# Sample tokens' expert rows added at slabs 226 to 268 of each layer in place of 226 to 284

## The chip, the cores and the metric

The kernel runs on one core of a Trainium2 chip. The metric is the device time of one execution in microseconds (us); the figure given is the median of 3 runs. The core's engines have names of their own in the profile: PE does matmuls (PEld loads their weights), DVE, ACT and POOL work on tiles, and SP issues DMAs. Each runs its own list of instructions in order and waits on semaphores for the others. 16 DMA engines move data between HBM and the on-chip memory for all queues together.

## The reference

Two layers of a hybrid decoder run over 256 prompt tokens and 32 sample tokens (8 sequences of 4), with 1024 channels, in float32. Each layer is a token mixer (a recurrent block in layer 0, a convolution block in layer 1) and then a PEER channel mixer, which picks 128 of 16,384 experts for every token (8 heads by 16) and adds up their rows of a table V, weighted:

```python
def expert_block(args):
    xblk, iblk, gblk = args
    u = jnp.take(u_tab, iblk, axis=0)
    act = jax.nn.gelu(jnp.einsum('ted,td->te', u, xblk).astype(jnp.float32))
    w = (gblk * act).astype(xblk.dtype)
    v = jnp.take(v_tab, iblk, axis=0)
    return jnp.einsum('te,ted->td', w, v)
```

## The kernel before

**The stream.** All weights and both expert tables flow through the core once, as 592 slabs of 128x1024 float32 (0.52 MB), 296 per layer: 16 for the mixer's input, 8 for its output, 16 for the PEER queries, 128 of U, 128 of V. `layer_slabs` (L60) sets their order: slabs 40 to 135 are U, then come 32 of V and 32 of U, and from slab 200 to 295 only V. The V slabs are read in visits, mostly of two slabs for two rows of experts; the visits of the last two of three blocks of experts begin at slabs 200 and 264 (`BLOCK_START[1]`, `BLOCK_START[2]`). For the prompt tokens every expert is computed densely and weighted by a gate that is zero where it was not picked.

**One slab.** SP issues its DMA into one of 3 buffers of `land` (L446), once the slab three before has been split. ACT makes the upper part `w_hi` (`split`, L583), DVE the rest `w_lo` (`split_lo`, L1470; POOL at L533 for a few early slabs), both in rings of 4. PE multiplies w_hi and w_lo with the weights `g_hi` and `g_lo`: 12 matmuls of 128x512 per V slab (`v_slab`, L909 to L911). ACT rounds g_hi for a visit (L783), DVE makes g_lo (L1745). The loops of ACT and DVE run over the slabs r of a layer. At r they split slab r + 3, and they make g_hi and g_lo of a visit at the r just before its first slab: w_lo is made three slabs ahead of PE, g_lo one.

**The gates.** DVE makes one-hot tiles for a few tokens at a time (`onehots`, L1592 and L1597), PE expands them into gates (`expand`, L956), DVE multiplies these into `hidden` (`apply`, L1609). `gate_schedule` (L115) spreads 64 such chunks a layer; those of the last block fall on slabs 200 to 242.

**The sample tokens.** Their picks don't go through the dense gates. Each layer has 32 adds (`SMP`): in add k, each of 128 partitions takes one picked row of V, 1024 wide, times its weight, and adds it to `smp_acc` (`add_sample`, L1659; the first is L1668, the others L1671). The rows come by `fetch_samples` (L505) on POOL: two indirect DMAs a row, one per half (L524), into 7 buffers in `hidden`. Rows 0 to 6 wait until a visit has freed their buffer (DVE's g_lo of that visit), each later row k waits for add k - 7. On POOL layer 0's `wide_weights` (L495) stand behind the last fetch. The adds are placed by the list `ADD_AT` (L150); in DVE's loop over r they come last:

```python
for r in range(first, SLABS):
    while applied < GATES and ONEHOTS_AT[applied] + 2 <= r: ...   # apply
    if r + 1 in VISITS: ...                                       # g_lo of the next visit
    split_lo(base + r + LEAD)
    while made < GATES and ONEHOTS_AT[made] <= r: ...             # onehots
    while fetched < SMP and ADD_AT[fetched] <= r:
        add_sample(L, fetched)
        fetched += 1
```

At slab 285 (`SMP_SUM`) PE sums `smp_acc` over partitions, at slab 287 (`SMP_OUT`) DVE adds the sum to x. Neither place depends on ADD_AT.

**Beside it.** At slab 264 of layer 0 ACT issues two DMAs for layer 1, the keys and the convolution states, 2 MB together (L806, L807). In layer 1 there are none.

Of the kernel before, what the change touches and what calls it, by code (L numbers as in the profile page):

```python
# [83 lines left out]
SLABS = len(LAYER)  # L84
# [10 lines left out]
def block_of(r):  # L95
    return next(b for b, (lo, hi) in enumerate(BLOCKS) if lo <= LAYER[r][2] < hi)


BLOCK_START = [min(r for r in V_AT if block_of(r) == b) for b in range(len(BLOCKS))]
# [46 lines left out]
STORE_LAG = 7  # L146
SMP_LANDS = 7
ACC_SLOT, LAND_SLOT, YT_SLOT = 32, 36, 72
ADD0, ADD1 = BLOCK_START[1] + 26, SLABS - 12
ADD_AT = [ADD0 + k * (ADD1 - ADD0) // (SMP - 1) for k in range(SMP)]  # L150
SMP_SUM, SMP_OUT = SLABS - 11, SLABS - 9
TURN_LATE = SLABS - TWICE
# [1734 lines left out]
```

How the kernel before makes its waits and increments, by code:

```python
        @block.sync  # L439
        def _(sp):
            for n in range(TOTAL):
                if n >= LANDS:
                    ready, count = lo_ready(n - LANDS)
                    sp.wait_ge(ready, count)
                place = n // SLABS * SLABS + LAYER[n % SLABS][1]
                sp.dma_start(land[:, n % LANDS, :], stream[place]).then_inc(landed[n % LANDS], 16)
                if n == 0:
                    for k in range(4):
                        two = slice(2 * k, 2 * k + 2)
                        sp.dma_start(x[:, two, :], x0[:, two, :]).then_inc(x_in[k], 16)
                        if k == 0:
                            sp.dma_start(cols[:, :], cols_d).then_inc(loaded, 16)
                for c in range(CH):
                    if n == SLABS + IN0 + 2 * c + 8:
                        sp.wait_ge(packed, c + 1)
                        sp.dma_start(cfs_d[:, c], packs[c]).then_inc(stored, 16)
                L, r = divmod(n - STORE_LAG, SLABS)
                if r in U_INDEX and U_INDEX[r] % GROUP == GROUP - 1:
                    e = U_INDEX[r] - GROUP + 1
                    for k in range(2):
                        sp.wait_ge(evacuated[k], L * USES + USE_U + U_INDEX[r] // 2 + 1)
                    at = e % STAGE
                    sp.dma_start(act_d[L][:, e:e + GROUP, :], smp_stage[:, at:at + GROUP, :]
                                 ).then_inc(smp_stored[at // GROUP], 16)
# [144 lines left out]
                def used(r):  # L609
                    act.wait_ge(slab_used, base + r + 1)
```

## Time and profile before

| what | value |
|---|---|
| median of 3 runs | 2098.67 us (2096.07 to 2100.24) |
| the profiled execution's own time | 2098.75 us |
| its span, first to last instruction | 2096.9 us |
| granted TensorE clock, mean | 0.995 |
| PE busy | 2055.7 us (98% of the span) |
| DVE busy | 1635.7 us (78%) |
| ACT busy | 960.7 us (46%) |
| POOL busy | 339.8 us (16%) |
| DMA traffic | 358.34 MB, mean 171 GB/s |

The median is the number to predict; the profile is one execution of the same program. Times in a trace row are us from the span's start, and a name such as L1671 is a line of the kernel. `w_lo<-land,w_hi` reads: written from land and w_hi. Buffers that lie in `hidden` (row buffers, smp_acc) have that name. A row's bracket gives the idle time just before it and what ended that. Layer 0's slab 226 is met by DVE at about 820 us, layer 1's at about 1882 us.

### The profile page before, as it was taken

Reading aid. Unit: us, or ns where it says so; the run is one execution under the profiler, and the core shown is the slowest. Engines: PE = TensorE matmul, PEld = TensorE weight load, DVE = VectorE, ACT = ScalarE, POOL = GpSimd, SP = SyncE. Lnnn points to the kernel's source line nnn. Section 1 sums busy time; section 2 is a strip of 40 time slices with the busy share of each in tenths; the row PEclk is TensorE's granted clock in tenths of the full one; section 3 lists DMA queues with packets and bytes.
Section 4 is the critical chain, followed back from the end, with each engine's and each line's share of the span. In section 5 each row is a group of like instructions: output and inputs, shape, how many; then the busy total and the mean of one; then the engine's idle time right before and its main releaser. Section 6 shows DMA issues by size and latency. Waiting matters only on the chain.

```text
span 2096.9 us, 40394 instructions
## 1 busy us (share of the span) xinstructions
PE 2055.7 (98%) x16458; PEld 1889.3 (90%) x16458; DVE 1635.7 (78%) x3068; ACT 960.7 (46%) x1642; POOL 339.8 (16%) x245
## 2 busy tenths in 40 slices
PE   8999999999999999999999999999999999999998
PEld 7899999999889988887897999999998899888886
DVE  7887995555887688978799779965557777789776
ACT  5654553344433343445655545533334433444443
POOL 0014000000000064642110050000000000456420
PEclk9999999999999999999999999999999999999999
DMA  5354554444554457897322435544445544567873
GB/s 180 111 156 130 178 158 157 154 154 157 171 171 147 145 163 233 293 316 230 125 90 65 145 123 163 170 156 154 148 157 172 171 147 147 163 228 259 301 245 103
DMA packets 112935, 358.34 MB, mean 171 GB/s; under 512 B 17264, under 2 KB 27760, under 8 KB 112496
## 3 DMA queue, kind: packets, MB, share of 16 engines
q1 hardware_dynamic: 99888, 319.99, 47.2%
q0 software_dynamic: 12288, 33.60, 4.9%
q8 instruction: 131, 2.15, 0.4%
q10 hardware_dynamic: 576, 2.18, 0.3%
q14 instruction: 52, 0.43, 0.1%
HBM read 349.09 MB, written 6.63 MB: 170 GB/s over the span
## 4 chain that ended last, share of the span: by engine, by line
PE 84%; DVE 12%; ACT 2%; issue 2%; DMA 1%; SPq 0%; DVEq 0%; ACTq 0%
PE ps L878 15%; PE ps L879 14%; PE ps L880 14%; PE ps L909 11%; PE ps L910 10%; PE ps L911 10%; PE ps L956 6%; DVE w_lo L1470 2%; DVE work L1356 2%; DMA land<-stream_dram 1%; ACT w_hi L583 1%; PE ps L1037 1%; DVE hidden L1356 1%; DVE work L1364 0%; DVE hidden L1376 0%
## 5 line engine op out<-in xcount | busy, mean ns | idle before, releaser
L1470 DVE TENSOR_TENSOR w_lo<-land,w_hi 128x1024 fp32r<-128x1024 f32 x562 | 684.8, 1219 | 275.3 <-ACT w_hi L583 274.7
L583 ACT CAST w_hi<-land 128x1024 fp32r<-128x1024 f32 x592 | 621.2, 1049 | 441.1 <-PE ps L911 351.0
L878 PE MATMUL ps<-act_hi,w_hi 128*128 128x288 f32 x2688 | 809.2, 301 | 12.8 <-DVE act_lo L1196 5.9
L879 PE MATMUL ps<-act_hi,w_lo 128*128 128x288 f32 x2688 | 794.9, 296 | 0.0
L880 PE MATMUL ps<-act_lo,w_hi 128*128 128x288 f32 x2688 | 791.9, 295 | 0.0
L878 PEld LDWEIGHTS ps<-act_hi,w_hi 128*128 128x128 f32 x2688 | 505.4, 188 | 18.4 <-issue 10.9
L880 PEld LDWEIGHTS ps<-act_lo,w_hi 128*128 128x128 f32 x2688 | 507.7, 189 | 0.0
L879 PEld LDWEIGHTS ps<-act_hi,w_lo 128*128 128x128 f32 x2688 | 506.7, 188 | 1.0
L909 PE MATMUL ps<-w_hi,g_hi 128*128 128x512 f32 x1024 | 404.9, 395 | 3.6 <-DVE g_lo L1745 3.6
L910 PE MATMUL ps<-w_lo,g_hi 128*128 128x512 f32 x1024 | 399.1, 390 | 0.0
L911 PE MATMUL ps<-w_hi,g_lo 128*128 128x512 f32 x1024 | 398.8, 389 | 0.0
L827 ACT ACTIVATE hidden<-ps 128x256 f32<-128x256 f32 x256 | 98.3, 384 | 497.9 <-PE ps L880 497.6
L512 POOL DMA_INDIRECT smp_act<-act_d,smp_idx x64 | 77.8, 1215 | 1108.3 <-DMA act_d<-smp_stage 1089.4
L909 PEld LDWEIGHTS ps<-w_hi,g_hi 128*128 128x128 f32 x1024 | 192.2, 188 | 44.3 <-DVE w_lo L1470 3.4
L911 PEld LDWEIGHTS ps<-w_hi,g_lo 128*128 128x128 f32 x1024 | 192.2, 188 | 40.6
L910 PEld LDWEIGHTS ps<-w_lo,g_hi 128*128 128x128 f32 x1024 | 192.4, 188 | 37.8
L524 POOL DMA_INDIRECT hidden<-stream_dram,smp_idx x128 | 170.9, 1335 | 162.1 <-DVE hidden L1671 91.1
L1592 DVE TENSOR_TENSOR work<-work 128x512 bf16<-128x512 bf16 (+2 forms) x256 | 164.5, 684 | 0.0
L1609 DVE TENSOR_TENSOR hidden<-ps,hidden 128x512 f32<-128x512 f32 x128 | 88.2, 689 | 95.4 <-PE ps L956 94.4
L956 PEld LDWEIGHTS ps<-work 128*128 128x128 bf16 x4608 | 131.2, 97 | 23.0 <-issue 14.1
L956 PE MATMUL ps<-work 128*128 128x32 bf16 (+1 forms) x4608 | 145.1, 182 | 2.3 <-DVE work L1597 2.3
L1597 DVE TENSOR_TENSOR work<-work 128x512 bf16<-128x512 bf16 x384 | 139.2, 416 | 0.0
(214 smaller groups left out, 1353.8 us busy)
## 6 DMA issues: line engine op xcount, KB each, us to landing
land<-stream_dram SPq DMA_DIRECT2D x592, 512.0 KB
act_d<-smp_stage SPq DMA_DIRECT2D x64, 64.0 KB, 3.3
hidden<-stream_dram,smp_idx POOLq DMA_INDIRECT x128, 5.5
x<-x_dram SPq DMA_DIRECT2D x4, 288.0 KB, 6.8
y_t_dram<-hidden SPq DMA_DIRECT2D x8, 144.0 KB, 1.9
work<-keys_dram SPq DMA_DIRECT2D x1, 1024.0 KB, 7.5
smp_act<-act_d,smp_idx POOLq DMA_INDIRECT x64
work<-keys_dram ACTq DMA_DIRECT2D x1, 1024.0 KB, 9.0
```

The costliest lines, as they stand in the source:

```text
L524: nc.gpsimd.indirect_dma_start(out=smp_land[buf][:, half * 512:half * 512 + 512], out_offset=None, in_=rows, in_offset=bass.IndirectOffset ...
L583: nc.scalar.copy(w_hi[:, m, :], land[:, n % LANDS, :]).then_inc(w_hi_ready, 1)
L878: nc.tensor.matmul(out, w_hi[:, slot, wsl], hi, start=start, stop=False)
L879: nc.tensor.matmul(out, w_lo[:, slot, wsl], hi, start=False, stop=False)
L880: return nc.tensor.matmul(out, w_hi[:, slot, wsl], lo, start=False, stop=stop)
L909: nc.tensor.matmul(out, g_hi[:, ring + ii, tok], w_hi[:, m, row], start=first and ii == 0, stop=False)
L910: nc.tensor.matmul(out, g_hi[:, ring + ii, tok], w_lo[:, m, row], start=False, stop=False)
L911: return nc.tensor.matmul(out, g_lo[:, ring + ii, tok], w_hi[:, m, row], start=False, stop=last and ii == 1)
L956: mm = nc.tensor.matmul(ps[:, GBANK + g % 2, t * n:(t + 1) * n], of_token(j, t), of_token(terms[k], t), start=(k == 0), stop=(k == TERMS - 1))
L1470: V.tensor_tensor(w_lo[:, k, :], land[:, n % LANDS, :], w_hi[:, k, :].bitcast(F32), ALU.subtract).then_inc(lo_by_dve, 1)
L1592: did(V.tensor_tensor(out, keys_of.unsqueeze(1).to_broadcast(shape), per_token(picks_b[:, kind, tok], shape), ALU.is_equal))
L1597: ins = V.tensor_tensor(terms[k], mask, per_token(gate_terms[:, k, tok], shape), ALU.mult)
```

## The change

The end of the range over which the adds are spread moves from 284 to 268; its beginning stays at 226, the number of adds at 32. So ADD_AT was 226, 227, 229, 231, 233, 235, 237, 239, 240, 242, 244, 246, ..., 284 and becomes 226, 227, 228, 230, 231, 232, 234, 235, 236, 238, 239, 240, 242, 243, 244, 246, ..., 268. The fetches from row 7 on hang on the adds and move with them.

```diff
@@ -146,7 +146,7 @@
 STORE_LAG = 7
 SMP_LANDS = 7
 ACC_SLOT, LAND_SLOT, YT_SLOT = 32, 36, 72
-ADD0, ADD1 = BLOCK_START[1] + 26, SLABS - 12
+ADD0, ADD1 = BLOCK_START[1] + 26, SLABS - 28
 ADD_AT = [ADD0 + k * (ADD1 - ADD0) // (SMP - 1) for k in range(SMP)]
 SMP_SUM, SMP_OUT = SLABS - 11, SLABS - 9
 TURN_LATE = SLABS - TWICE
```

## Rows read from the trace of the kernel before

**Rows 1.** The page: PE's busy time, DMA queue q0, the chain that ended last.

```profile
PE 2055.7 (98%) x16458; PEld 1889.3 (90%) x16458; DVE 1635.7 (78%) x3068; ACT 960.7 (46%) x1642; POOL 339.8 (16%) x245
...
q0 software_dynamic: 12288, 33.60, 4.9%
...
PE 84%; DVE 12%; ACT 2%; issue 2%; DMA 1%; SPq 0%; DVEq 0%; ACTq 0%
```

**Rows 2.** Windows, PE alone: stretch, us, busy (matmuls), clock, DMA share, GB/s.

```profile
819.50:882.00 62.50, 62.24 (x566) 1.00 0.74 259
...
932.00:950.00 18.00, 15.43 (x67) 1.00 0.88 330
...
1881.00:1944.00 63.00, 62.73 (x572) 1.00 0.75 258
...
1994.00:2012.00 18.00, 18.00 (x81) 1.00 0.87 282
```

**Rows 3.** Windows, busy PE, PEld, DVE, ACT, POOL; clock, DMA share, GB/s last.

```profile
905.00:932.00 27.00, 27.00 (x121) 22.36 (x120) 22.49 (x22) 13.12 (x15) 12.35 (x11) 1.00 0.90 297
...
1967.00:1994.00 27.00, 27.00 (x121) 22.37 (x120) 21.68 (x21) 13.13 (x15) 12.88 (x11) 1.00 0.89 312
```

**Rows 4.** The chain that ended last, 930 to 951 us: start, us, what.

```profile
935.01 10.89 DMA land<-stream_dram
```

**Rows 5.** Timeline of ACT, 840 to 965 us: start, us, instruction, idle before.

```profile
929.98 0.35 ACTq L806 DMA_DIRECT2D work<-keys_dram  x1
...
938.20 1.05 ACT L583 CAST w_hi<-land 128x1024 fp32r<-128x1024 f32 x1 [4.47 <-DMA land<-stream_dram]
```

**Rows 6.** DMA queues, 930 to 944.25 us: packets, MB, share of 16 engines.

```profile
q1 hardware_dynamic: 555, 2.05, 38.6%
q10 hardware_dynamic: 288, 2.03, 36.6%
q0 software_dynamic: 398, 1.29, 24.4%
```

**Rows 7.** Groups by line and form, DVE, 819.5 to 882 us: busy, mean ns, idle before.

```profile
L1470 DVE TENSOR_TENSOR w_lo<-land,w_hi 128x1024 fp32r<-128x1024 f32 x20 | 24.3, 1218 | 0.8 <-ACT w_hi L583 0.8
...
L1745 DVE TENSOR_TENSOR g_lo<-hidden,g_hi 128x512 fp32r<-128x512 f32 x10 | 6.8, 679 | 0.0
```

**Rows 8.** Timeline of DVE, layer 0, slabs 226 to 248.

```profile
849.18 1.28 DVE L1671 SCALAR_TENSOR_TENSOR hidden<-hidden,smp_act 128x1024 f32<-128x1024 f32 x1
...
865.82 1.27 DVE L1671 SCALAR_TENSOR_TENSOR hidden<-hidden,smp_act 128x1024 f32<-128x1024 f32 x1
867.01 0.68 DVE L1609 TENSOR_TENSOR hidden<-ps,hidden 128x512 f32<-128x512 f32 x1
867.61 0.68 DVE L1745 TENSOR_TENSOR g_lo<-hidden,g_hi 128x512 fp32r<-128x512 f32 x1
...
878.83 0.68 DVE L1745 TENSOR_TENSOR g_lo<-hidden,g_hi 128x512 fp32r<-128x512 f32 x1
...
882.08 1.23 DVE L1470 TENSOR_TENSOR w_lo<-land,w_hi 128x1024 fp32r<-128x1024 f32 x1 [1.43 <-ACT w_hi L583]
```

**Rows 9.** The chain that ended last, 858 to 870 us, at slab 242.

```profile
868.44 0.47 PE ps L909
```

**Rows 10.** Timeline of PE, first matmuls of slabs 245 and 246, layer 0.

```profile
878.03 0.39 PE L909 MATMUL ps<-w_hi,g_hi 128*128 128x512 f32 x1
...
880.75 0.39 PE L909 MATMUL ps<-w_hi,g_hi 128*128 128x512 f32 x1
```

**Rows 11.** Timeline of DVE, layer 1, a pair of slabs past slab 246.

```profile
1949.27 1.23 DVE L1470 TENSOR_TENSOR w_lo<-land,w_hi 128x1024 fp32r<-128x1024 f32 x1 [1.28 <-ACT w_hi L583]
```

**Rows 12.** Timeline of POOL, layer 0, the two fetches of row 7.

```profile
832.42 5.59 POOL L524 DMA_INDIRECT hidden<-stream_dram,smp_idx  x1 [0.30 <-issue]
838.32 0.94 POOL L524 DMA_INDIRECT hidden<-stream_dram,smp_idx  x1 [0.30 <-issue]
```

**Rows 13.** All row fetches (L524) by line: from issue to landing.

```profile
DMA to landing us min/median/max: 3.6/5.5/10.8
```

## The prediction

> **What bounds the kernel now.** I read the page first: PE is busy for 98% of the span and makes 84% of the chain that ended last, DVE 12% of it [rows 1]. So a change on DVE, POOL or the DMA queues costs or gives time only where PE stands still, and PE's busy time by stage is the next view [rows 2]. In the stages in which a layer's 32 sample rows are added PE is whole but for two kinds of place. From 819.5 to 882 us (slabs 226 to 246 of layer 0) 62.24 of 62.50 us are busy, in layer 1's same slabs 62.73 of 63.00: some 0.3 lost. From 932 to 950 us only 15.43 of 18 are, and this exists in layer 0 alone: the same 18 us of layer 1 hold 81 matmuls, those of layer 0 hold 67 [rows 2]. The 14 that are missing, at 27 us for 121 matmuls [rows 3], are 3.1 us. That is nearly all that this change can give back.
>
> The chain says what PE waits for there: 10.89 us of it, from 935.01 on, is a landing of land [rows 4]. ACT issues the keys of layer 1 at 929.98, the conformer states right behind, and its w_hi at 938.20 had waited 4.47 us for its slab [rows 5]. In the 14.25 us from 930 on the stream's queue q1 moved 2.05 MB, keys and states (q10) 2.03, the sample rows (q0) 1.29 [rows 6]: 5.37 MB, 377 GB/s.
>
> The first kind of place is DVE's. In 819.5 to 882, where the one-hots of the last gate block are still made, its groups stand almost back to back: 20 w_lo with 0.8 us of idle time before them in all, 10 g_lo with none [rows 7]. An add takes 1.20 us of the queue (865.82 to the next start at 867.01). g_lo of slab 242 starts at 867.61, and the matmuls that need it at 868.44, at once when it is there [rows 8, 9]: 0.83 us from start to start where PE waits. g_lo of slab 246 starts at 878.83, that slab's matmuls at 880.75 [rows 8, 10], so it has a lead of 880.75 - 878.83 - 0.83 = 1.1 us. A slab takes 2.72 us (878.03 to 880.75) [rows 10].
>
> **The change part by part.** One constant moves, so the last add stands at slab 268 and not 284, and the 32 adds are 42/31 = 1.35 slabs apart and not 58/31 = 1.87. Nothing is added or removed: 32 adds and 64 row fetches a layer, as before. Three things follow.
>
> *DVE in slabs 226 to 246.* In program order 11 adds stand ahead of g_lo of slab 246 now (those at slabs up to 244), 15 after. Four more at 1.20 are 4.8 us. The 0.8 us in which DVE waited for ACT [rows 7] are filled first; of the 4.0 that are left the lead hides 1.1, and PE starts slab 246 2.9 us later. Queued behind an add are the next g_lo and w_lo, and PE waits for g_lo, made one slab ahead, long before it would for w_lo, made three ahead. Layer 1 loses the same 0.3 us in these slabs [rows 2], so I take the same there: 5.8 us for two. Bounds: if slab 248 decided, at a like lead, the 1.43 us that DVE waits before 882.08 [rows 8] would be filled too, 1.4 per layer; if no idle time were filled, 3.7. I take 2.9, the slab with the greatest excess before that idle time. Past slab 246 the one-hots are over and DVE waits 1.28 us in each pair of slabs [rows 11]; there are 1.48 adds per pair in place of 1.07, 0.5 us more, which fits.
>
> *The keys of layer 0.* They go at slab 264, unmoved. Row fetches run seven adds ahead: the last is issued after the 25th add, now at slab 270, then at 258. So the 1.29 MB of q0 leave the 14.25 us. The stream needs 14.25/2.72 slabs of 0.524 MB, 2.75 MB; it had 2.05 and could have 3.34 [rows 6]. I give back 2.6 of the 3.1 us and leave 0.5 for landings still slowed by q10. Bounds 0 and 3.1.
>
> *The DMA engines in slabs 246 to 258.* A row is two of 128 fetches that carry 33.6 MB [rows 1], 0.525 MB, as much as a slab. Now the demand is 1.53 slabs per 2.72 us, 296 GB/s, and the trace shows 297 at a share of 0.90; then it is 1.74 slabs, 335 GB/s, for 12 slabs. No row has just that. The nearest is 312 GB/s at 0.89 with PE whole [rows 3], so nothing is lost there; the other way lies the 3.1 us stall, with the stream starved. Bounds 0 and 3.1 per layer; I take 0.5, since 312 is near and 335 is between.
>
> The Trainium skill, DMA: Bandwidth & Descriptors, Specifications, gives a limit of some 358 GB/s from HBM per core. The trace is above it, 377 over 14.25 us [rows 6], so the measurement decides; by the page 335 would still fit and this term would be an estimated 0, while the share of 0.90 at 297 [rows 3] would have the engines full at 330 and the term at its upper end.
>
> *What costs nothing.* POOL's fetches end some ten slabs sooner, and with them layer 0's wide weights behind them, which still wait for slab 263 and which layer 1 alone reads. SP's order stays; its stream issues wait for w_lo, so DVE's lateness passes to them, inside the room that w_lo has. The sum over the samples on PE stays at slab 285; nothing was late for it, so an earlier last add gives nothing.
>
> Sum: the profiled execution took 2098.75 us, 0.08 over the median of the runs. 2098.75 + 5.8 + 2 x 0.5 - 2.6 = 2102.95, against the median 2102.9: 4.2 us slower, which is just 0.2% (about what a measurement of this kernel can tell from no change). So "slower" and "the same" are near to even.
>
> **Rivals.**
> *Not slower: the lead holds.* If the buffers ahead of PE take up the overload of DVE wherever it falls, only the keys' stall changes: 2098.75 - 2.6 = 2096.2. For it: w_lo is made three slabs ahead, and PE loses only 0.3 us in the stretch [rows 2]. Against: g_lo, one slab ahead, held PE at 868.44 already [rows 9]. It decides at slabs 242 to 246: whether PE starts them without a wait. 10%.
>
> *The stream starves in slabs 246 to 258.* The share reaches 1.0 and each layer pays the upper bound: 2098.75 + 5.8 + 6.2 - 2.6 = 2108.1. For it: 0.90 at 297 [rows 3]. Against: 377 in rows 6. 9%.
>
> *Rows come late, and DVE waits in an add with g_lo behind it.* Row 7's two fetches took POOL from 832.42 to 839.26, one of them 5.59 us where the other takes 0.94, while DVE was full [rows 12]; landings take 5.5 us in the median, 10.8 at most [rows 13]. So row 7 is there at 844.8; its add moves to slab 235, where one ran at 849.18 [rows 8], and two more adds ahead of it make that 851.6. That is 6.8 us in hand. But eight rows (7 to 14) at 6.84 us of POOL each would bring row 14 at 832.42 + 54.7 + 5.5 = 892.6, and its add, the last before g_lo of slab 246, is due near 881.6 (878.83 + 4.0 - 1.2): 11 us per layer in place of the 2.9, 2098.75 + 22 - 2.6 = 2118. Against: one such fetch is no pattern. 4%.
>
> The Trainium skill, SBUF — State Buffer, Who interferes with whom, says that a DVE instruction with two SBUF inputs contends with a GpSimd one that reads SBUF. The 5.59 us [rows 12] may be that, which no run here shows; more adds would then bring more such waits and the time would go towards this rival's 2118.
>
> *It does not do what it says.* The first seven fetches hang on buffers that a visit's g_lo frees, not on adds, and a DVE that is late spreads the adds by itself: 2098.7, 5%.
>
> **Numbers.** The forecast, 2102.9, has 72%: by its bounds 38 of them slower by over 0.2%, 34 within. The rivals of the stream and the rows add 9 and 4 to slower; the lead that holds gives 7 to the same and 3 to faster, the last rival 5 to the same. Slower 0.51, same 0.46, faster 0.03. The range: 1.4 per layer with all of the 3.1 back gives 2098.5, and it starts at 2098.6, which leaves out the lead that holds; upward 3.7 per layer with the other terms as taken gives 2104.6, and it reaches on to the starved stream, 2108.1.
>
> **What would show it.** Right: PE waits for g_lo several times between slabs 230 and 246 in both layers, 2.5 to 3.5 us in each, with no idle time on DVE there; the stretch after the keys' issue loses under 1 us; DVE has more idle time after slab 268, and PE gains nothing from it. Wrong: PE whole in slabs 226 to 246 (the lead held); w_hi late by microseconds for landings in slabs 246 to 258, with PE behind it (the stream starves); gaps on DVE ahead of adds that end with a landing (rows late); a stall at the keys as long as now.

## The result, and the profile after the change

The changed kernel takes **2111.4 us** in the median of 4 runs (2110.61 to 2113.35), the kernel before 2098.7 in 4 runs beside it (2096.07 to 2100.24): a ratio of 1.0063, with an interval of 1.0046 to 1.0081. It is slower by some 13 us; the forecast was 4, and the range ended at 2108.1. The profiled execution has a span of 2109.9 us against 2096.9, at a mean granted clock of 0.996 against 0.995, so the profile shows the same 13.0 us.

First the page of the changed kernel: busy times, the chain that ended last, the group of the row fetches (busy and mean ns, then the idle time before it).

```profile
PE 2058.0 (98%) x16458; PEld 1888.3 (89%) x16458; DVE 1636.9 (78%) x3068; ACT 960.7 (46%) x1642; POOL 370.2 (18%) x245
...
PE 76%; DVE 12%; DMA 4%; POOL 3%; issue 2%; ACT 2%; SPq 0%; DVEq 0%; ACTq 0%
...
L524 POOL DMA_INDIRECT hidden<-stream_dram,smp_idx x128 | 198.6, 1552 | 84.1 <-DVE g_lo L1745 46.9
```

PE's share of the chain has gone from 84% to 76% [rows 1]. DMA has gone from 1% to 4% there, and **POOL, which was not in the chain at all, holds 3%**. POOL is busy for 370.2 us in place of 339.8 with the same 245 instructions. An engine that issues the same work and is busy 30 us longer has been held up inside its instructions.

To see where the 13 us went I cut PE's timeline at the first matmul of slabs 226, 246, 267 and 272. These are the four matmuls of layer 0, timeline of PE (start us, us, instruction):

```profile
814.90 0.39 PE L909 MATMUL ps<-w_hi,g_hi 128*128 128x512 f32 x1
...
884.02 0.47 PE L909 MATMUL ps<-w_hi,g_hi 128*128 128x512 f32 x1
...
942.60 0.39 PE L909 MATMUL ps<-w_hi,g_hi 128*128 128x512 f32 x1
...
960.66 0.39 PE L909 MATMUL ps<-w_hi,g_hi 128*128 128x512 f32 x1
```

Call the three stretches A (slabs 226 to 246, where one-hots are still made), B (246 to 267) and C (267 to 272, where the keys of layer 1 arrive). Here A takes 884.02 - 814.90 = 69.12 us. The same cut of both kernels, us, layer 0 / layer 1:

| stretch | PE never waiting | before | after | after less before |
|---|---|---|---|---|
| A, 226 to 246 | 63.69 | 64.24 / 64.29 | 69.12 / 69.64 | +4.88 / +5.35 |
| B, 246 to 267 | 57.12 | 57.12 / 57.35 | 58.58 / 58.99 | +1.46 / +1.64 |
| C, 267 to 272 | 13.60 | 16.72 / 13.60 | 18.06 / 13.60 | +1.34 / 0 |

The sum is 14.7 us. Layer 0's slab 200, ahead of anything that the change touches, began 1.6 us earlier in this execution (732.2; over the twelve profiles of this study that start lies between 732.2 and 734.7), and 14.7 - 1.6 - 0.1 elsewhere is the 13.0 of the spans. So A costs 10.2, B 3.1, C 1.3. ("PE never waiting" is what a run below with short adds took.)

**Stretch A.** DVE's groups by form in 818 to 882 us of the changed kernel (busy, mean ns, idle time before):

```profile
L1470 DVE TENSOR_TENSOR w_lo<-land,w_hi 128x1024 fp32r<-128x1024 f32 x19 | 23.1, 1217 | 0.2 <-ACT w_hi L583 0.2
L1671 DVE SCALAR_TENSOR_TENSOR hidden<-hidden,smp_act 128x1024 f32<-128x1024 f32 x14 | 17.9, 1276 | 1.9 <-DMA hidden<-stream_dram,smp_idx 1.9
```

Against [rows 7], the 0.8 us in which DVE waited for w_hi are down to 0.2: DVE is full, as forecast. But it has a new idle time of 1.9 us, ahead of an add and ended by a landing. The timeline of DVE has it:

```profile
868.93 1.28 DVE L1671 SCALAR_TENSOR_TENSOR hidden<-hidden,smp_act 128x1024 f32<-128x1024 f32 x1 [1.92 <-DMA hidden<-stream_dram,smp_idx]
870.13 0.68 DVE L1609 TENSOR_TENSOR hidden<-ps,hidden 128x512 f32<-128x512 f32 x1
870.74 0.68 DVE L1745 TENSOR_TENSOR g_lo<-hidden,g_hi 128x512 fp32r<-128x512 f32 x1
```

The add of row 11 waits for its row, the g_lo of slab 242 stands behind it on DVE, and PE behind that g_lo. Why the row is late is told by the chain that ended last, 838 to 900 us (start, us, what):

```profile
840.84 6.24 POOL hidden L524
847.08 0.30 issue
847.38 0.95 POOL hidden L524
848.33 0.30 issue
848.64 1.97 POOL hidden L524
850.61 0.30 issue
850.92 4.50 POOL hidden L524
855.42 0.30 issue
855.73 2.63 POOL hidden L524
858.35 0.30 issue
858.66 1.43 POOL hidden L524
860.09 0.30 issue
860.39 8.52 DMA hidden<-stream_dram,smp_idx
868.93 1.28 DVE hidden L1671
```

For these 20 us nothing but POOL sets the end: it issues row fetches one behind the other, with 0.3 us between them, and single ones take 2 to 6 us where the shortest take 0.94. The twelve fetches of rows 6 to 11, counted from the start of the first (828.77) to the start of the thirteenth (865.80), take 37.0 us; the same twelve took 25.4 before.

What a slow fetch waits for can be read beside DVE's timeline. These are the adds that start last before the ends of the three longest fetches (847.08, 855.42, and 865.50 for one that started at 860.39):

```profile
846.18 1.27 DVE L1671 SCALAR_TENSOR_TENSOR hidden<-hidden,smp_act 128x1024 f32<-128x1024 f32 x1
...
854.52 1.28 DVE L1671 SCALAR_TENSOR_TENSOR hidden<-hidden,smp_act 128x1024 f32<-128x1024 f32 x1
...
864.60 1.28 DVE L1671 SCALAR_TENSOR_TENSOR hidden<-hidden,smp_act 128x1024 f32<-128x1024 f32 x1
```

Each fetch ends 0.90 us after the start of the add. So it is in all twelve profiles of this study: 99 row fetches took over 2.1 us; 84 of them end 0.90 us after the start of an add or of an apply, and 15 end 0.8 us after the end of a w_lo behind which DVE came to a pause. No fetch stays open more than 0.91 us past the start of an add. What holds a fetch is thus a run of w_lo, g_lo and one-hots without a pause; an add lets it through. DVE's pauses inside the twelve fetches are 0.17 us in all in the kernel before and none here. Where in DVE's queue each fetch falls, and why other, short fetches get through between one-hots, is open.

**Stretch B.** The waits in 815 to 1020 us, layer 0's stretches and what follows (total us, times, longest):

```profile
PE ps L909 <- DVE g_lo L1745: 7.2, 7, 2.6
...
DVE hidden L1671 <- DMA hidden<-stream_dram,smp_idx: 2.2, 2, 1.9
...
POOL hidden L524 <- DVE hidden L1671: 0.3, 1, 0.3
```

The last line is the telling one. Before, POOL waited for adds 48.1 us in layer 0 (17 times), so the adds set its pace; the same line of the kernel before, 815 to 1020 us:

```profile
POOL hidden L524 <- DVE hidden L1671: 48.1, 17, 8.4
```

Now it waits 0.3 us. POOL is late, and when DVE has gaps again from about 870 us on it issues the remaining 20 rows back to back, bunched into some 60 us. What that does to the DMA engines, in windows (us, PE's busy time, granted clock, DMA share, GB/s):

```profile
884.00:929.00 45.00, 44.09 (x194) 1.00 0.98 354
...
1954.00:1996.00 42.00, 40.81 (x178) 1.00 0.98 356
```

They are full, at a share of 0.98 in both layers, where [rows 3] had about 0.9 at some 300 GB/s. In those 45 us of layer 0 the queues moved:

```profile
q1 hardware_dynamic: 2275, 8.28, 51.8%
q0 software_dynamic: 2314, 7.60, 46.2%
```

At full pace 45 us are 45/2.72 = 16.5 slabs of 0.524 MB, 8.67 MB; the stream got 8.28. It starves. The waits of w_hi for landings in B of layer 0, here (884 to 942 us) and in the kernel before (881 to 938):

```profile
ACT w_hi L583 <- DMA land<-stream_dram: 20.3, 13, 2.7
```

```profile
ACT w_hi L583 <- DMA land<-stream_dram: 5.6, 3, 2.1
```

PE, which lost 0 and 0.2 us in B before, loses 1.5 and 1.9.

**Stretch C.** ACT's timeline:

```profile
934.74 0.35 ACTq L806 DMA_DIRECT2D work<-keys_dram  x1
...
943.81 1.05 ACT L583 CAST w_hi<-land 128x1024 fp32r<-128x1024 f32 x1 [5.35 <-DMA land<-stream_dram]
```

Against [rows 5] w_hi waits 5.35 us behind the keys and not 4.47. The last row fetch started at 928.4, 6 us ahead of the keys, and from the keys' issue on q0 moves nothing for 14.25 us. What the stream moves in these (934.74 to 948.99 us):

```profile
q1 hardware_dynamic: 627, 2.25, 41.9%
```

It had 2.05 MB there with the rows beside it [rows 6]. So the rows' bytes are gone, and still the stall is longer. What they leave behind is a stream that has nothing in reserve: for the five slabs up to 934.73 w_hi waited 1.0 to 1.9 us for each landing, where in the kernel before it waited for PE. PE then waited 2.59 us for a g_lo, and after that wait its clock fell. Windows of PE, as above:

```profile
944.00:948.00 4.00, 1.48 (x7) 1.00 0.66 243
948.00:952.00 4.00, 3.93 (x12) 0.68 0.53 185
```

A whole window holds 17 or 18 matmuls. From 948 to 952 PE is busy and does 12: from 949.58 to 952.57 its matmuls start 0.43 us apart in place of 0.23, which is the lower of the two levels (1.2 GHz). The ten steps from 949.29 to 953.16 take 3.87 us where 2.27 were due, so the clock costs 1.6 of C's 4.5 us over full pace.

### The profile page after: what moved, and what is told of

Read it like the earlier page. It is cut to its first block, busy times and chain, and to the rows that moved or that the text cites. A ratio compares the mean times of both kernels' runs of the same rounds, so it can differ in the third digit from the quotient of the medians.

```text
span 2109.9 us, 40394 instructions
## 1 busy us (share of the span) xinstructions
PE 2058.0 (98%) x16458; PEld 1888.3 (89%) x16458; DVE 1636.9 (78%) x3068; ACT 960.7 (46%) x1642; POOL 370.2 (18%) x245
## 3 DMA queue, kind: packets, MB, share of 16 engines
q0 software_dynamic: 12288, 33.60, 4.6%
## 4 chain that ended last, share of the span: by engine, by line
PE 76%; DVE 12%; DMA 4%; POOL 3%; issue 2%; ACT 2%; SPq 0%; DVEq 0%; ACTq 0%
PE ps L878 15%; PE ps L880 14%; PE ps L879 14%; PE ps L909 8%; PE ps L910 8%; PE ps L911 8%; PE ps L956 5%; POOL hidden L524 3%; DMA land<-stream_dram 3%; DVE w_lo L1470 2%; DVE work L1356 2%; ACT w_hi L583 1%; DMA hidden<-stream_dram,smp_idx 1%; PE ps L1037 1%; DVE hidden L1671 1%
## 5 line engine op out<-in xcount | busy, mean ns | idle before, releaser
L524 POOL DMA_INDIRECT hidden<-stream_dram,smp_idx x128 | 198.6, 1552 | 84.1 <-DVE g_lo L1745 46.9
```

What stands on the lines that cost most here:

```text
L524: nc.gpsimd.indirect_dma_start(out=smp_land[buf][:, half * 512:half * 512 + 512], out_offset=None, in_=rows, in_offset=bass.IndirectOffset ...
```

## The experiments

The theory after this reading: (1) four more adds among the one-hots fill DVE; (2) a DVE without gaps holds up POOL's row fetches, so that rows are late and adds wait with g_lo behind them; (3) POOL, behind, then issues its rows in a bunch that starves the stream in B and leaves it without a reserve for the keys in C. The rivals: the adds alone cost all of A; the rows are late because of their bytes in the DMA engines; the keys alone make C; and, for (2), that the adds themselves, not the fullness, hold POOL up. What each run gave, us, layer 0 / layer 1:

| run | time, ratio to before [interval] | A | B | C |
|---|---|---|---|---|
| before | | 64.24 / 64.29 | 57.12 / 57.35 | 16.72 / 13.60 |
| after | 2111.4, 1.0063 [1.0046, 1.0081] | 69.12 / 69.64 | 58.58 / 58.99 | 18.06 / 13.60 |
| e1: 12 adds left in place | 2098.6, 1.0006 [0.9997, 1.0016] | 64.30 / 64.25 | 59.31 / 57.63 | 14.68 / 13.60 |
| e3: before, 7 rows | 2095.3, 0.9984 [0.9975, 0.9994] | 64.26 / 64.25 | 57.12 / 57.12 | 14.81 / 13.60 |
| e2: after, 7 rows | 2100.9, 1.0014 [1.0005, 1.0024] | 67.06 / 67.07 | 57.20 / 57.24 | 13.94 / 13.60 |
| e6: after, narrow rows | 2104.0, 1.0027 [1.0016, 1.0037] | 68.25 / 67.08 | 57.25 / 57.24 | 13.93 / 13.60 |
| e7: after, short adds | 2093.7, 0.9983 [0.9974, 0.9993] | 63.69 / 63.69 | 57.12 / 57.12 | 13.60 / 13.60 |
| e10: after, short one-hots | 2095.9, 0.9986 [0.9976, 0.9995] | 63.69 / 63.69 | 57.12 / 57.12 | 14.90 / 13.60 |
| e4: after, keys at 280 | 2108.0, 1.0048 [1.0032, 1.0065] | 70.49 / 68.34 | 58.31 / 58.78 | 13.87 / 13.60 |
| e5: before, keys at 280 | 2095.5, 0.9992 [0.9983, 1.0001] | 64.28 / 64.27 | 57.12 / 57.12 | 13.60 / 13.60 |
| e8: last add at 276 | 2103.1, 1.0025 [1.0014, 1.0037] | 65.25 / 65.22 | 58.83 / 57.12 | 17.45 / 13.60 |
| e9: 7 adds among one-hots, keys at 280 | 2094.7, 0.9987 [0.9978, 0.9996] | 63.71 / 63.71 | 57.12 / 57.12 | 13.60 / 13.60 |

A, B and C are of one execution of each kernel. The changed kernel and e4 run the same instructions in A, and theirs differ by 1.4 and 1.3 us, so a single A of a kernel with late rows is no surer than that.

### e1: the first twelve adds where they were

```diff
-ADD0, ADD1 = BLOCK_START[1] + 26, SLABS - 28
-ADD_AT = [ADD0 + k * (ADD1 - ADD0) // (SMP - 1) for k in range(SMP)]
+ADD0, ADD1 = BLOCK_START[1] + 26, SLABS - 12
+ADD_AT = [ADD0 + k * (ADD1 - ADD0) // (SMP - 1) for k in range(12)] + [
+    ADD0 + 21 + (k - 12) * 21 // 19 for k in range(12, SMP)]
```

> Adds 0 to 11 at their old slabs (226 to 246), the other 20 between 247 and 268. Three stretches of PE are compared, from first matmul to first matmul, layer 0 / layer 1: A from slab 226 to 246 (kernel before 64.24 / 64.29 us, changed kernel 69.13 / 69.65), B from 246 to 267 (57.12 / 57.35; 58.57 / 58.99), C from 267 to 272 (16.72 / 13.59; 18.06 / 13.59). If the loss in A comes from more adds among the one-hots (by DVE's queue, by late rows, or by both), A is back at 64.3. If A's loss comes from a fuller DMA in general, A stays over 66. If bunched row fetches starve the stream, B gets worse than in the changed kernel, 60 or more, since 20 adds fall on 22 slabs; if not, B is 57.3. Sum by the first: some 2105 us, under the 2111.4 of the changed kernel.

A is back at 64.3 in both layers, though the last add stands at slab 268 as in the changed kernel. So all of A's loss comes from adds that moved in among the one-hots, and none from the earlier end as such. The price is only moved: twenty adds from 247 to 268 pack the rows tighter still, and B stands 2.2 us over full pace in layer 0 and 0.5 in layer 1 (under the 60 that was given), while C, with the last fetch out at 924.8, gains 2.0. The sum is no difference from the kernel before; the 2105 given for it was 6 us too high.

### e3 and e2: the adds without the rows

Both kernels fetch only seven rows a layer; all 32 adds run, on those.

```diff
-                for k in range(SMP):
+                for k in range(SMP_LANDS):
...
-                dve.wait_ge(smp_landed[k % SMP_LANDS], 32 * (L * len(range(k % SMP_LANDS, SMP, SMP_LANDS)) + k // SMP_LANDS + 1))
+                dve.wait_ge(smp_landed[k % SMP_LANDS], 32 * (L + 1))
```

> The kernel before with only rows 0 to 6 fetched in each layer (25 of 32 rows left out of the sample tokens' sum), the adds at their old slabs. The counterpart of the run with seven rows on the changed kernel (A 67.06 / 67.07, B 57.20 / 57.24, C 13.94). If the rows' bytes make the keys' stall here too, C is 13.9 and not 16.72. A is 64.3 if the 0.3 us lost there are DVE's program order, 64.0 if the rows had a part. The difference in A between the two, 2.8 us, is then the price of four more adds among the one-hots alone. Sum some 2095.5.

> The changed kernel, but only rows 0 to 6 are fetched in each layer; adds 7 to 31 run at their new slabs on what lies in the buffers (25 of the 32 rows are left out of the sample tokens' sum). No add waits for a landing past row 6, and q0 is quiet. If DVE's program order alone makes the loss in A, A is 69 or more as in the changed kernel. If my term of 2.9 per layer was right and the rest was late rows, A is 67.2 (64.3 + 2.9). If late rows were all of it, A is 64.3. B: 57.1 if row fetches starved the stream, 58.5 or more if DVE was the cause. C in layer 0: 14 or less if the rows made the keys' stall, 16.5 or more if keys and states do that by themselves.

This isolates DVE's own price. Without late rows, the new places cost 67.06 - 64.26 = 2.8 us in layer 0 and 2.8 in layer 1, the forecast's 2.9. PE loses it in layer 0 of e2 at slabs 230, 232, 234, 238 and 242, in waits of 0.2 to 0.5 us for g_lo, and once, 0.5 us, for a one-hot; at slab 246 it doesn't wait. The other 2.1 to 2.6 us of A in the changed kernel (69.12 and 69.64 less 67.06) exist only with the rows. B and C stand near full pace in e2: with no rows' traffic the keys cost 0.3 us. In e3 they cost 1.2 without rows (C 14.81, where 13.9 was given).

### e6: the same fetches with 1/32 of the bytes

```diff
-                rows = stream.rearrange("s p (two w) -> (s p two) w", two=2)
+                narrow = stream.rearrange("s p (k w) -> (s p k) w", w=16)
...
-                            out=smp_land[buf][:, half * 512:half * 512 + 512], out_offset=None, in_=rows,
+                            out=smp_land[buf][:, half * 512:half * 512 + 16], out_offset=None, in_=narrow,
```

> The changed kernel with each fetch cut from 512 to 16 columns of its 128 rows (the sample tokens' sum is left without 31 of 32 parts of each V row): POOL makes as many descriptors, q0 moves a 32nd of the bytes. If POOL, held up while DVE is full, is what brings rows late, A stays at 69 or more and DMA_INDIRECT still takes 4 to 6 us in places. If the landings are slow because the DMA engines are full, A falls to some 67.2. B: 57.1 if the bytes of the rows starved the stream. C: 14 or less if the rows' bytes made the keys' stall, 16.5 or more if not.

The view of line 524's instructions (duration in ns, least/median/most; issue to landing), of e6 and then of the changed kernel:

```profile
L524 POOL DMA_INDIRECT hidden<-stream_dram,smp_idx x128: 940/1143/6245, 788.7 to 1985.9; - x128
...
DMA to landing us min/median/max: 2.5/3.8/6.1
```

```profile
L524 POOL DMA_INDIRECT hidden<-stream_dram,smp_idx x128: 940/1168/6246, 788.2 to 1997.0; - x128
...
DMA to landing us min/median/max: 3.5/5.8/10.3
```

POOL's durations don't care for bytes: 6.245 us at most against 6.246, and again 37.0 us for the twelve fetches. What the bytes change is the landing, 3.8 us in the median against 5.8. (q0 has 1.09 MB and 6144 packets in all there, in place of 33.60 and 12,288.) So the slow issue is not the DMA engines'. Row 11's add still waits in layer 0, 1.08 us in place of 1.92; in layer 1 none does, and A is e2's there, 67.08. In this execution A's second part thus shrinks with the landings. But it is the fastest of e6's eight (2100.1 us, median 2104.0), and that median lies 3.1 us over e2's: what the others lost no profile shows, and how much of A the long landings cost stays open. B is at 57.25 here, as without rows: its loss was the rows' bytes.

### e7: adds of 16 columns in place of 1024

```diff
-                    V.scalar_tensor_tensor(out=smp_acc, in0=smp_land[k % SMP_LANDS], scalar=w, in1=smp_acc,
-                                           op0=ALU.mult, op1=ALU.add).then_inc(smp_added, 1)
+                    V.scalar_tensor_tensor(out=smp_acc[:, 0:16], in0=smp_land[k % SMP_LANDS][:, 0:16], scalar=w,
+                                           in1=smp_acc[:, 0:16], op0=ALU.mult, op1=ALU.add).then_inc(smp_added, 1)
```

> The changed kernel with adds 1 to 31 on 16 of 1024 columns (98 in 100 of the sample tokens' sum are left out); all rows are fetched whole. If POOL's slow fetches (4 to 6 us) come from a full DVE, they shrink to 2 us or less while DVE has gaps, row 11 is not late, and A is 64.3 or less. If POOL is slow because its DMA queue is full, the fetches stay at 4 to 6 us. B and C: the rows then come as soon as their buffers are free, so if their bytes starve the stream B stays over 57.5 and C depends on whether they are over before the keys at slab 264: 14 to 18.

DVE's groups in 819.5 to 882 us and PE's windows of e7:

```profile
L1470 DVE TENSOR_TENSOR w_lo<-land,w_hi 128x1024 fp32r<-128x1024 f32 x21 | 25.6, 1220 | 9.8 <-ACT w_hi L583 9.8
...
L1671 DVE SCALAR_TENSOR_TENSOR hidden<-hidden,smp_act 128x16 f32<-128x16 f32 x14 | 3.2, 230 | 0.0
```

```profile
818.00:882.00 64.00, 64.00 (x580) 1.00 0.82 287
882.00:942.00 60.00, 60.00 (x266) 1.00 0.92 326
```

With gaps on DVE (9.8 us before w_lo alone) no fetch takes over 2.6 us (2 was given), the twelve take 20.6, and PE loses nothing in A, B and C, although every row's bytes move and the adds stand where the change put them. The second window matters most: evenly paced rows at 326 GB/s and a share of 0.92 cost PE nothing, and the keys, still at slab 264, cost nothing either. With short adds the whole loss of the change is gone; that it takes long one-hots as well, the next run shows.

### e10: whole adds, short one-hots

e7 took away the fullness and the adds together, so the last run keeps the adds and shortens other work.

```diff
+                some = GTOK[b] // 2 if b < 2 else 1
-                tok = slice(c * GTOK[b], (c + 1) * GTOK[b])
+                tok = slice(c * GTOK[b], c * GTOK[b] + 2 * some)
...
-                    did(V.tensor_tensor(out, keys_of.unsqueeze(1).to_broadcast(shape),
+                    did(V.tensor_tensor(out[:, 0:some], keys_of.unsqueeze(1).to_broadcast(shape),
...
-                    ins = V.tensor_tensor(terms[k], mask, per_token(gate_terms[:, k, tok], shape), ALU.mult)
+                    ins = V.tensor_tensor(terms[k][:, 0:some], mask[:, 0:some], per_token(gate_terms[:, k, tok], shape), ALU.mult)
```

> The changed kernel, but the one-hots of the last gate block (slabs 200 to 242 of each layer) are made for 2 of the 16 tokens of a chunk, so that part of the gates is left out; the adds stay whole and where the change put them, and the fetches stay whole. It tells apart what the short adds could not: whether POOL's row fetches are held up because DVE has no gaps in slabs 226 to 242, or by the adds themselves (1.2 us each, two inputs in the on-chip memory), which short adds took away together with the fullness. DVE loses some 14 of its 64 us between slabs 226 and 246 here. Theory of the gaps: the 12 row fetches from row 6 on, which took POOL 37.0 us in the changed kernel and 17.5 with short adds, take under 24 (those 12 took 23.9 before the change); no add waits for a landing; slabs 226 to 246 take PE 63.7 to 64.0 us in both layers, 246 to 267 57.1 to 57.6, 267 to 272 13.6 to 14.2; the time is 2094 to 2096. Theory of the adds: the 12 fetches still take over 30 us, row 11 lands as late as in the changed kernel though DVE is early for it, adds wait for landings by 2 us and more several times, and the stages after slab 246 stay at 58.5 and 14 to 18; the time is 2099 to 2105.

Two numbers in that text were counted one or two fetches short: to the start of the thirteenth fetch the twelve take 25.4 us before the change and 20.6 with short adds (37.0 in the changed kernel stands). The view of line 524 and DVE's groups (818 to 882 us) of e10, whose add is on line 1672:

```profile
L524 POOL DMA_INDIRECT hidden<-stream_dram,smp_idx x128: 942/947/3244, 788.6 to 1977.8; - x128
```

```profile
L1470 DVE TENSOR_TENSOR w_lo<-land,w_hi 128x1024 fp32r<-128x1024 f32 x21 | 25.6, 1220 | 6.4 <-ACT w_hi L583 6.4
L1672 DVE SCALAR_TENSOR_TENSOR hidden<-hidden,smp_act 128x1024 f32<-128x1024 f32 x14 | 17.9, 1281 | 0.0
...
L1610 DVE TENSOR_TENSOR hidden<-ps,hidden 128x512 f32<-128x512 f32 x7 | 4.8, 691 | 2.6 <-PE ps L956 2.6
```

Fourteen whole adds in the stretch, 17.9 us as in the changed kernel, but DVE has gaps (6.4 and 2.6 us before two of its groups): the twelve fetches take 20.3 us (828.74 to 849.01), no fetch over 3.24, no add waits for a row, and A and B are at full pace. It is the fullness that holds POOL up, not the adds. Whether the gaps did it or the shorter one-hots between the adds, e10 can't tell apart: of its eight fetches over 2.1 us six end at an add and two at a gap. One number missed: C is 14.90 in layer 0, over the 14.2 given. The keys at slab 264 can still cost 1.3 us with the last fetch started at 918.7; in e7, with the last at 918.6, they cost nothing, and in e3, without rows, 1.2. What decides between 0 and 1.3 was not settled.

### e4 and e5: the keys at slab 280

```diff
-                    if r == BLOCK_START[2] and L == 0:
+                    if r == BLOCK_START[2] + 16 and L == 0:
```

> The changed kernel with the keys and states of layer 1 issued at slab 280 of layer 0 in place of 264, where no row fetch is left. A and B as in the changed kernel. C is 13.6 in layer 0. If row fetches made the stall, the keys now cost under 1 us around slab 284 and the sum is some 4 us under the changed kernel (2107.5); if keys and states starve the stream by themselves, 3 us or more are lost there and the sum is within 1.5 us of it.

> The kernel before with only the keys and states of layer 1 moved from slab 264 to 280 of layer 0, past its last row fetch (958 us). Stretches as before: A (slab 226 to 246), B (246 to 267), C (267 to 272). If row fetches make the keys' stall, as the run with the keys at 280 on the changed kernel says, C falls from 16.72 to some 13.9 in layer 0, nothing new is lost past it, A and B stay at 64.3 and 57.1 to 57.4, and the sum is 2.5 to 3 us under the kernel before (about 2095.3). If the keys cost the same wherever they stand, it is within 1 us of it.

With the keys away from the rows C is at 13.87 after the change and 13.60 before it. So the rows alone cost 0 to 0.3 us in C, the keys alone 0 to 1.3 (e2, e3, e7, e10), and the 3.1 before the change and the 4.5 after it need the keys together with rows, beside them or just ahead of them. In the kernel before, that gives all 3.1 us of [rows 2] back in the profile; the ratio, 0.9992, has 1.7 us of it, with an interval that reaches 1. In the changed kernel it gives 4.2 of 18.06. Of A, which was to stay, layer 1 is shorter, 68.34, and layer 0 longer, 70.49: there PE waits 2.65 us for the g_lo of slab 242, and the clock falls behind that wait:

```profile
870.00:874.00 4.00, 2.15 (x5) 0.67 0.68 197
```

The changed kernel has the like wait at the like place, 2.57 us, and its granted clock stayed 1.00.

### e8: the last add at slab 276

```diff
-ADD0, ADD1 = BLOCK_START[1] + 26, SLABS - 28
+ADD0, ADD1 = BLOCK_START[1] + 26, SLABS - 20
```

> Half the move: the last add at slab 276, 12 adds ahead of the weights of slab 246 where there were 11 and are 15 in the changed kernel. By the term of the forecast (adds x 1.20, less 0.8 of idle time, less the lead of 1.1) one more add costs nothing or a few tenths: A 64.3 to 65. If the price were the same for each add, A would be 65.5. B: 57.1 to 58. C stays at 16 or more, as rows still come at slab 264. Sum within 2 us of the kernel before.

Twelve adds stand ahead of g_lo of slab 246 here, one more than before, and A grows by 1.0 and 0.9 us. By the forecast's own working one add, 1.20 us, would have been swallowed by 0.8 of idle time and a lead of 1.1; PE waits at slabs 232 and 244 and for a one-hot at 240, and not at 246. No add waits for a row in A, but the twelve fetches take 38.2 us already (no pause of DVE falls inside them), and the bunch behind them costs 1.7 in B, over the 58 given, and 0.7 in C of layer 0; in layer 1, where they take as long, B loses nothing. The sum, given within 2 us of the kernel before, is 5 over it. So there is no room for even one more add.

### e9: fewer adds among the one-hots

From these runs the opposite of the change should help: seven adds three slabs apart while one-hots are made, the others behind, and the keys after them. The edit is made to the kernel before.

```diff
-ADD_AT = [ADD0 + k * (ADD1 - ADD0) // (SMP - 1) for k in range(SMP)]
+ADD_AT = [ADD0 + 3 * k for k in range(7)] + [ADD0 + 20 + (k - 7) * 38 // 24 for k in range(7, SMP)]
...
-                    if r == BLOCK_START[2] and L == 0:
+                    if r == BLOCK_START[2] + 16 and L == 0:
```

> A version that should beat both kernels: only 7 adds (in place of 11) ahead of the weights of slab 246, three slabs apart, the other 25 from slab 246 to 284, and the keys and states at slab 280. If what the runs so far show holds (a full DVE slows POOL's fetches, rows then bunch), DVE has gaps in A and A falls to 63.7 as with the narrow adds, 0.55 us under the kernel before in each layer; C is 13.6 to 14, 3 us less. Against it: 25 adds on 39 slabs ask for 1.63 slabs' bytes per slab, over the 1.53 now, and if that starves the stream B and C lose over 1 us per layer. Sum 2094 by the first, 2096.5 or more by the second.

PE's windows of e9:

```profile
818.00:884.00 66.00, 66.00 (x588) 1.00 0.69 233
884.00:946.00 62.00, 62.00 (x276) 1.00 0.90 310
```

PE is whole through both stretches; A is 63.71, B and C are at full pace. At 2094.7 us, a ratio of 0.9987 [0.9978, 0.9996], it beats both kernels, by little: the kernel before lost only 0.6 us a layer in A and 3.1 in C.

## Why the prediction was wrong

The direction was right and the largest term too; the miss is 8.8 us of span (13.0 against 4.2), and but for a part in C it comes from one assumption.

**"DVE in slabs 226 to 246": right as a size.** The forecast was 2.9 us a layer. The adds alone cost 2.8 (e2 less e3). The place was wrong, and that the size came out is in part luck. The working took slab 246, with four more adds and a lead of 1.1. In e2 PE waits at slabs 230 to 242 and not there. Slab 242 has twelve adds ahead of its g_lo and had nine, and no lead, since PE waited for it before [rows 9]: 3 x 1.20 - 0.8 = 2.8. The fourth add and the lead, 1.20 and 1.1, all but cancel. e8 charges 1.0 us for the first add more, which the lead at slab 246 and the idle time should have hidden.

**"Row fetches run seven adds ahead": the step that failed.** It stands in "The keys of layer 0" and was carried, unsaid, into the DMA term. It holds while the adds set POOL's pace, as they did before (48.1 us of waiting). With DVE full of w_lo, g_lo and one-hots POOL was the slower of the two and ran 11.6 us behind its former pace over twelve fetches (37.0 less 25.4). Three losses follow:

- In A, rows come late: 69.12 and 69.64 less 67.06 and 67.07, 4.6 us for both layers, which the sum did not have. The rival of the late rows had the mechanism, down to g_lo behind the waiting add, with 4%. It priced every row at 6.84 us of POOL and came to 11 a layer; twelve fetches took 37.0, so a row took 6.2, but that shortfall met a margin and became one or two waits of 0.9 to 1.9 us: 2.3 a layer.
- In B, the term was 0.5 a layer and measured 1.5. The demand at an even pace would have been carried at no cost (e7, 326 GB/s); bunched rows fill the engines to 0.98. The rival of the starving stream had this, at 3.1 a layer.
- In C, the term was a gain of 2.6 and became a loss of 1.3. Here a second step failed, that the stream "had 2.05 and could have 3.34". The rows' bytes did leave the 14.25 us behind the keys' issue, as forecast, but the stream did not get them: it moved 2.25 MB in the changed kernel, and 2.12 in e7, where PE lost nothing. What e7 had was a stream ahead of PE when the keys came (w_hi had last waited for PE, 1.66 us). In the changed kernel the bunch had used that up, and w_hi waited for landings. With POOL on pace the gain is there: e7 gives all 3.1 back, e10 1.8. The longer wait of PE also brought the lower clock, 1.6 us, of which the forecast had no term.

Together 4.6 + 2.1 + 3.9, with their decimals 10.7, less 0.2 on DVE's term and less 1.7 of this execution's earlier start and rest: the 8.8.

The rivals of a holding lead and of an edit without effect fell: PE waited for g_lo seven times in layer 0. Of the four signs that the prediction named as proof against it, three are in the profile: w_hi late for landings behind slab 246, a gap on DVE ended by a landing, a stall at the keys no shorter than before. [Rows 12] showed a fetch of 5.59 us while DVE was full, and calling it "no pattern" was the error. The same trace has it a second time, at the same place of layer 1:

```profile
1894.13 5.58 POOL L524 DMA_INDIRECT hidden<-stream_dram,smp_idx  x1 [0.30 <-issue]
```

The page that the prediction put beside that row, the Trainium skill, SBUF — State Buffer, Who interferes with whom, says that GpSimd's way to the on-chip memory is one that DVE shares, and that a DVE instruction with two inputs there contends with a GpSimd instruction that reads there. The trace agrees in part. w_lo, g_lo and the one-hots have two such inputs, and back to back they hold a fetch for up to 6.2 us; an apply, with one of its inputs in ps (where PE writes), lets it through. But an add, which has two such inputs as well, also lets it through, 0.90 us after its start. So the rule alone does not sort DVE's instructions here, and which way in the hardware is fought over no run shows.

On the DMA engines, [rows 6] had 377 GB/s over 14.25 us, which the prediction set against the limit of some 358 that the Trainium skill, DMA: Bandwidth & Descriptors, Specifications, states. In the two long bunches the engines were full at 354 and 356, just under the page's figure. But in [rows 6] they were full too, the three queues' shares making 99.6%, and carried 377. What full engines carried thus changed with the mix of transfers, and that the page's limit bound the bunches is not shown. The prediction's other reading, engines full at 330, was too low.

## What to carry to other kernels

When work is packed denser on one engine, ask what the engines that feed it need of its gaps: a producer that was paced by the consumer may be slowed by it, and then its output comes late first and bunched afterwards. A single odd duration in the trace of before is worth a closer look when it lies where the resource is already as full as the change will make it elsewhere: see whether it comes again at the like place, and what starts on the other engines just before it ends. A stream with prefetch should be costed at the pace its producer can hold, not at the order that its semaphores allow. And bytes that leave a stretch are not a gain by themselves: look at how far ahead the stream stands when the stretch begins.

## What the runs showed of the hardware

POOL's indirect fetch takes 0.94 us at least. While DVE runs w_lo, g_lo and one-hots back to back it stays open, up to 6.25 us, whatever it moves (6.245 with 64 bytes for each partition, 6.246 with 2 KB). Of the 99 fetches over 2.1 us in the twelve profiles 84 end 0.90 us after the start of an add or an apply on DVE, and 15 where DVE pauses. The longest takes 3.24 us where DVE has gaps of some 9 us in 64 (e10), 2.58 with 11 (e7), and 5.59 with 4.4 (e9). Why an add lets a fetch through, these runs don't tell.

The granted clock fell to its lower level after a PE wait of 2.59 us at slab 268 of the changed kernel and after one of 2.65 at slab 242 of e4, each time for some microseconds (0.68 and 0.67 in the window behind it), and not after one of 2.57 at slab 242 of the changed kernel or of 2.56 at slab 268 of e8. A wait of this length can thus cost another 1.6 us, or nothing; what decides it these runs don't tell.
